# Triangular solves by halves: chunk blocks of 64 in partition halves, products in quadrants of the array

## What is computed

```python
def step(state, inp):
    r_t, w_t, k_t, v_t, kk_t, a_t = inp
    sa = jnp.einsum('bhij,bhj->bhi', state, -kk_t)
    state = (state * w_t[:, :, None, :] + sa[..., None] * (kk_t * a_t)[:, :, None, :]
             + v_t[..., None] * k_t[:, :, None, :])
    return state, jnp.einsum('bhij,bhj->bhi', state, r_t)
```

## Time and profile before

| | |
|---|---|
| runs of the kernel | 4231.69, 4227.73, 4236.51 us (median 4231.69) |
| the profiled execution | 4219.72 us, its span 4217.9 us |
| busy: PE, PEld, DVE, ACT, POOL | 91%, 78%, 63%, 38%, 15% of the span |
| granted TensorE clock, mean | 0.974 of 2.4 GHz |
| `rwkv_core` in layer 0 | 1966.1 to 2070.1 us of the span |
| `rwkv_core` in layer 1 | 3125.6 to 3223.9 us of the span |

### The profile page before, as it was taken

One profiled execution on the slowest core, in us unless ns is written; L12 is line 12 of the kernel. 1 busy time (PEld: TensorE's weight loads), 2 busy tenths in 40 slices (PEclk: granted clock), 3 DMA queues, 4 the chain that ended last, 5 costly groups with the idle time before them and its releaser, 6 DMA issues. The chain is left out here.

```text
span 4217.9 us, 62645 instructions
## 1 busy us (share of the span) xinstructions
PE 3827.2 (91%) x23712; PEld 3274.3 (78%) x23712; DVE 2652.3 (63%) x5252; ACT 1614.2 (38%) x3540; POOL 629.5 (15%) x665
## 2 busy tenths in 40 slices
PE   6999998999999999998999889888889998998887
PEld 4788765788788867897878888777778788887776
DVE  6878556677755556555346666776563476677774
ACT  3222536322332345442225444444322254444443
POOL 1100000000000000000000144444300001444442
PEclk9999998999999999998999999999999999999999
DMA  5554211354433311542033699999820346999998
GB/s 213 201 189 169 77 40 51 106 193 165 136 138 131 129 72 33 199 180 100 21 130 137 240 419 419 420 419 419 371 80 27 124 150 251 419 419 419 419 419 336
DMA packets 135053, 905.05 MB, mean 215 GB/s; under 512 B 14855, under 2 KB 15879, under 8 KB 35168
## 3 DMA queue, kind: packets, MB, share of 16 engines
q0 software_dynamic: 95552, 620.97, 36.5%
q1 hardware_dynamic: 39200, 280.08, 18.5%
HBM read 899.90 MB, written 5.28 MB: 215 GB/s over the span
## 5 line engine op out<-in xcount | busy, mean ns | idle before, releaser
L2533 PE MATMUL ps<-arena 128*128 128x128 f32 x6560 | 845.7, 285 | 155.9 <-ACT arena L2597 154.8
L2533 PEld LDWEIGHTS ps<-arena 128*128 128x128 f32 x6560 | 795.0, 197 | 217.9 <-ACT arena L2597 212.4
L2688 DVE CUSTOM_DVE_ANT_0 arena<-arena 128x1024 f32<-128x1024 f32 x410 | 502.5, 1226 | 325.9 <-DMA arena<-peer_uv,arena 325.2
L630 DVE TENSOR_TENSOR w_lo<-wt,w_hi 128x1024 fp32r<-128x1024 f32 x388 | 475.2, 1225 | 327.4 <-ACT w_hi L612 302.1
L2660 POOL DMA_INDIRECT arena<-peer_uv,arena x410 | 441.4, 1077 | 1579.1 <-DVEq L2651 988.1
L665 PE MATMUL ps<-h_hi,w_hi 128*128 128x512 f32 (+1 forms) x1744 | 643.5, 371 | 30.9 <-DVEq L631 19.2
L612 ACT ACTIVATE w_hi<-wt 128x1024 fp32r<-128x1024 f32 x388 | 407.6, 1058 | 626.7 <-PE ps L665 598.1
L665 PE MATMUL ps<-h_hi,w_lo 128*128 128x512 f32 (+1 forms) x1744 | 635.4, 366 | 0.0
L665 PE MATMUL ps<-h_lo,w_hi 128*128 128x512 f32 (+1 forms) x1744 | 594.1, 368 | 11.7 <-DVE h_lo L759 10.8
L454 PE MATMUL ps<-hT,wt 128*128 128x256 f32 x1632 | 404.4, 385 | 4.8 <-DVE hT L543 3.8
L665 PEld LDWEIGHTS ps<-h_hi,w_hi 128*128 128x128 f32 x1744 | 332.4, 191 | 93.5 <-issue 23.3
(11 more groups left out here) (347 smaller groups left out, 5510.7 us busy)
## 6 DMA issues: line engine op xcount, KB each, us to landing
wt<-wstream SPq DMA_DIRECT2D x262, 1024.0 KB, 4.8
ada_t<-adastream POOLq DMA_DIRECT2D x133, 512.0 KB, 3.6
arena<-peer_uv,arena POOLq DMA_INDIRECT x410, 20.2
arena<-adastream POOLq DMA_DIRECT2D x11, 512.0 KB, 26.6
bias_by_query<-bias_by_distance POOLq DMA_DIRECT2D x1, 4096.0 KB, 16.7
arena<-bias_by_query POOLq DMA_DIRECT2D x1, 3072.0 KB, 11.8
xT<-tokens SPq DMA_DIRECT2D x1, 2048.0 KB, 15.2
cst<-consts SPq DMA_DIRECT2D x1, 1816.0 KB, 9.1
```

What stands on the lines that cost most here:

```text
L630: self.step(self.dve.tensor_tensor(lo, raw_group(g), hi.bitcast(F32), ALU.subtract))
L2533: ins = pe.matmul(y_banks(t)[m // 4][:, (m % 4) * P:(m % 4 + 1) * P], row[:, D + m * P:D + (m + 1) * P], diag[n % DIAGS], start=s == 0 and ...
L2688: dve.tensor_tensor_reduce(u, u, ztok[:, t], 1.0, 0.0, ALU.mult, ALU.add, hbuf[:, t, s:s + 1]).then_inc(dot_ready.sem, 1)
```

## The change

The two chunks of a tile are stored one under the other: chunk c of a chain lies in partitions 64c to 64c+63, so that a chain is 128 partitions x (4 heads x 64 columns), and the zero quarters are gone. Every product of a chain is then 8 matmuls of 64 x 64 x 64 (u = 0..3, c = 0, 1) instead of 4 of 128 x 128 x 128. Chunk c uses rows 64c.. and output partitions 64c.. of the array, a quadrant on its diagonal, and writes into the bank of its own: the rings CR_ and CD_ have two slots of two banks each, in place of four banks each. ACT and DVE take such a pair of banks out in two instructions of 64 partitions x 256 columns. The transpose becomes a matmul with XT as the stationary and the identity as the moving operand. A gram makes both g of a tile at once: 16 matmuls (32 records) where two grams had 4 (8 records) each. Masks have 64 columns. The masks that produce `lrb` and `lrk` still write the wide form, with the zeros (`masked_wide`), since the next stage reads them so. All buffers of the stage now lie in the arena. The table of constants that is loaded at the start is 384 columns narrower.

```diff
-    ("level", LEVELS * P), ("before", P), ("upto", P), ("window", QT * TOK), ("cmp", QT * N_CMP),
+    ("level", LEVELS * CH), ("before", CH), ("same", CH), ("upto", P), ("window", QT * TOK), ("cmp", QT * N_CMP),
...
+        CR_ = ring("core_a", [ps[:, 4:6], ps[:, 6:8]])
+        CD_ = ring("core_d", [ps[:, 0:2], ps[:, 2:4]])
+        ROWS = [slice(i * CH, (i + 1) * CH) for i in range(2)]
         CHAINS = [(t, g) for t in range(2) for g in range(2)]
-        LATER = [(name, c) for name in ("ka", "br", "kr") for c in CHAINS]
+        LATER = [(name, t) for name in ("ka", "br", "kr") for t in range(2)]
...
-            def gram(a, b, t, g):
-                for u in range(4):
-                    mm(bank[:, u * P:(u + 1) * P], a[r, u, t * P:(t + 1) * P], b[r, u, t * P:(t + 1) * P],
-                       inc=D_.full if u == 3 else None)
+            def gram(a, b, t):
+                for u in range(4):
+                    for c in range(2):
+                        x = slice(t * P + c * CH, t * P + (c + 1) * CH)
+                        for g, r in enumerate(ROWS):
+                            mm(banks[ROWS[c], g, u * CH:(u + 1) * CH], a[r, u, x], b[r, u, x],
+                               inc=CD_.full if u == 3 and c and g else None)
-            def into(r, a, b):
-                for u in range(4):
-                    mm(bank[:, u * P:(u + 1) * P], a[:, u, :], b(u), inc=r.full if u == 3 else None)
+            def by_rows(ring_of, a, b):
+                pe.wait_ge(ring_of.free, ring_of.given_back())
+                banks = ring_of.claim()
+                for u in range(4):
+                    for c, r in enumerate(ROWS):
+                        mm(banks[r, c, u * CH:(u + 1) * CH], a[r, u, :], b(u, c, r), inc=ring_of.full if u == 3 and c else None)
...
-                    ins = pe.transpose(bank[:, u * P:(u + 1) * P], XT[c[0]][c[1]][:, u, :], ident)
+                by_rows(CR_, XT[t][g], lambda u, c, r: ident[r, c * CH:(c + 1) * CH])
...
-                    into(A_, LTL[t][g], lambda u: X[t][g][:, u, :])
-                    if coming:
+                    by_rows(CR_, LTL[t][g], lambda u, c, r: X[t][g][r, u, :])
+                    if coming and i % 2:
...
-                    into(D_, Y[t][g], lambda u: XT[t][g][:, u, :])
+                    by_rows(CD_, Y[t][g], lambda u, c, r: XT[t][g][r, u, :])
...
-            def four_out(dst, ready):
-                step(act.activation(dst, bank.rearrange("p (a b) -> p a b", b=P), ACT.Copy))
+            def rows_out(dst, ready=None):
+                for c, r in enumerate(ROWS):
+                    ins = act.activation(dst[r], banks[r, c, 0:4 * CH].rearrange("p (u j) -> p u j", j=CH), ACT.Copy)
+                if ready:
+                    step(ins)
...
-                step(dve.tensor_tensor(dst, bank4(bank), four(const(mask)), ALU.mult))
+                for g in range(2):
+                    step(dve.tensor_tensor(dsts[g], banks[:, g, 0:4 * CH].rearrange("p (u j) -> p u j", j=CH),
+                                           four(const(mask)), ALU.mult))
...
-                step(dve.tensor_tensor(dst, dst, bank4(bank), ALU.add))
+                for c, r in enumerate(ROWS):
+                    ins = dve.tensor_tensor(dst[r], dst[r], banks[r, c, 0:4 * CH].rearrange("p (u j) -> p u j", j=CH), ALU.add)
+                step(ins)
```

More of the change, by code:

```diff
@@ L1704, in act_rwkv_core @@
-            for t, g in CHAINS:
-                act.wait_ge(A_.full, A_.filled())
-                bank = A_.take()
-                act.activation(by_group(utok, t)[:, :, g, :], bank[:, 0:256].rearrange("p (a b) -> p a b", b=HD),
-                               ACT.Copy).then_inc(A_.free, 1)
+                    rows_out(Y[t][g], act_ready)
+            for t in range(2):
+                for g in range(2):
+                    rows_out(W1[t][g], act_ready)
+                act.wait_ge(CR_.full, CR_.filled())
+                banks = CR_.take()
+                act.activation(xat[:, :, t, :].rearrange("p u (c j) -> p u c j", j=CH),
+                               banks[:, :, 0:4 * CH].rearrange("p c (u j) -> p u c j", j=CH), ACT.Copy).then_inc(CR_.free, 1)
@@ L1723, in added, with masked @@
-            def added(dst):
-                dve.wait_ge(D_.full, D_.filled())
-                bank = D_.take()
-                step(dve.tensor_tensor(dst, dst, bank4(bank), ALU.add))
-                dve.sem_inc(D_.free, 1)
+                return ap.unsqueeze(1).to_broadcast([P, 4, CH])
+            def masked(dsts, mask):
+                dve.wait_ge(CD_.full, CD_.filled())
+                banks = CD_.take()
+                for g in range(2):
+                    step(dve.tensor_tensor(dsts[g], banks[:, g, 0:4 * CH].rearrange("p (u j) -> p u j", j=CH),
+                                           four(const(mask)), ALU.mult))
+                dve.sem_inc(CD_.free, 1)
@@ new lines, in masked_wide @@
+            def masked_wide(dst, mask, t):
+                dve.wait_ge(CD_.full, CD_.filled())
+                banks = CD_.take()
+                wide = [P, 4, 2, CH]
+                for g in range(2):
+                    step(dve.tensor_tensor(
+                        dst[:, t, g::2].rearrange("p u (c j) -> p u c j", j=CH),
+                        banks[:, g, 0:4 * CH].rearrange("p (u j) -> p u j", j=CH).unsqueeze(2).to_broadcast(wide),
+                        const(mask).rearrange("p (c j) -> p c j", j=CH).unsqueeze(1).to_broadcast(wide), ALU.mult))
+                dve.sem_inc(CD_.free, 1)
@@ L1729, in level_of @@
+            def added(dst):
+                dve.wait_ge(CD_.full, CD_.filled())
+                banks = CD_.take()
+                for c, r in enumerate(ROWS):
+                    ins = dve.tensor_tensor(dst[r], dst[r], banks[r, c, 0:4 * CH].rearrange("p (u j) -> p u j", j=CH), ALU.add)
+                step(ins)
+                dve.sem_inc(CD_.free, 1)
             def level_of(t, g, level):
-                step(dve.tensor_tensor(LTL[t][g], LT[t][g], four(const("level", level, P)), ALU.mult))
+                step(dve.tensor_tensor(LTL[t][g], LT[t][g], four(const("level", level, CH)), ALU.mult))
```

124 lines of the change are left out of this document (49 added, 75 removed).

## The result

The change made the kernel faster by more than I forecast, and by more than my range allowed. The median after is 4176.55 us (4 runs, 4170.52 to 4179.04); that of before, with one more run, is 4233.94. The ratio is 0.9864, 95% interval 0.9847 to 0.9882. I had said 4211.

A forecast was written before the change was run, and what follows sets the result against it. A plain level was about half PE's, half DVE's. 79.0 us a layer plus 0.55 x 20.9 for half clock gave 181 for both layers against 202.4; saving 21.4 less 1.5, so 4211 us, range 4182 to 4236.

The forecast's parts named there:

- The sum at full clock: rwkv_core a layer: start-up 12.3, gram levels 39.6, plain level 10.9, level 5 7.1, tail 9.1; together 79.0 us.
- Which clock?: Step on PE's clock in rwkv_core: PE idles more often, so half clock for some 55% of the stage.
- the sign that I had named for being wrong: PEclk in the stage above 0.9 would show the forecast wrong; it expected near 0.7.
- the price that I put on half clock: rwkv_core wholly at half clock takes 99.9 us a layer against 79.0 at full, 20.9 more.
- rival (1): The clock holds: both layers of rwkv_core at 79.0, a saving of 44 us, kernel at 4187; chance 0.21.
- The 1.5 for `rwkv_out`: Next stage would begin at half clock where it now begins at full, taking 1.5 us off the saving.
- the difference of 12.0 between profile and median: Profiled execution of before, 4219.7, lies 12.0 us under the runs' median; the same difference was assumed after.
- The grams: Levels 1 to 3: 12 grams of 1.09 us in line become 6 of 1.06; 39.6 us against 49.5.
- (2): Rival: half clock throughout rwkv_core, 2 x 99.9 us, a saving of 2.6, kernel at 4229; chance 0.18.
- (4): Rival: the change does nothing because DVE is the bound; plain levels nearly so, 10.9 against 11.36; no separate chance.
- (3): Rival: the 0.033 us matmul rate fails; with half clock 148 us a layer, kernel at 4325; chance 0.09.
- the bound of 0.82 a product: Upper bound for a 16-record product at full clock, 0.82 us against 0.53 taken; some 3 us a level.

The follow-up runs named there:

- a_one_by_one: Kernel after, a product's eight matmuls ordered four of chunk 0, then four of chunk 1, so quadrants don't alternate; stage 84.8 and 84.0 us, kernel 4187.1.
- a_doubled: Kernel after, each product of turns, A and D products, W1 and u made twice into the same banks; stage 89.4 and 91.1 us, median 4198.9.
- a_idle: Kernel after, PE held ahead of each stage until ACT made 24 added copies; stage 77.8 and 76.9 us, kernel 4202.1.
- a_early_grams: Kernel after, a level's two grams moved behind the third and fourth turn ahead of it; stage 71.4 and 72.3 us, median 4164.0.
- a_events: Kernel after, levels and tail without engines waiting for their own copy, addition or mask before signalling; stage 67.5 and 71.0 us, median 4158.7.
- a_kept: Kernel after, three added matmuls of 128 columns ahead of each turn while PE waits for DVE; stage 88.7 and 92.9 us, median 4200.6.
- b_kept: Kernel before, two added matmuls of 512 columns in each of four start-up waits; stage 100.2 and 108.9 us, median 4225.3.

## Why the prediction was wrong

**The sum at full clock: right.** 79.0 us a layer forecast; 76.7 measured, with some 10.7 us at half clock in it. The product's 0.53 (0.50), ACT's 0.96, DVE's 0.84 and 1.66 all held. Four parts were off by over 1 us, in both directions and partly by where I cut them: the start-up (11.0 for 12.3), the gram levels (38.5 for 39.6), level 5 (8.5 for 7.1) and the tail (7.7 for 9.1). That their errors nearly cancel is in part luck.

**The step that failed: "Which clock?"** I wrote: "PE is idle more often, not less ... So I expect it at half clock for more of the stage than before, some 55%." It was 14% (10.7 of 76.7), in four stages of two profiles, at PEclk 0.93: the sign that I had named for being wrong, above 0.9, came true. a_one_by_one and a_doubled show that the inference does not carry: the one is busier than after at a lower clock, the other busier at a higher one. And the price that I put on half clock, 0.21 us for each us, was 0.08 in a_idle. I had written down the very rows (ACT's 0.96 and DVE's 1.66 against a product of 1.06) by which a slow PE hides, but priced only the first products of each row of four as if nothing could absorb them. In numbers: the forecast added 0.55 x 20.9 = 11.5 us a layer for the clock, 23 in both. At 0.08 the 21.4 us at half clock cost 1.7. This term made 21 of the missing 34.5 us. The share was the larger error: 0.14 x 20.9 would have been 2.9 a layer, at my own price. Why the clock held is not known. My rival (1), 4187, was this case, and I gave it 0.21.

**Smaller terms.** The full-clock sum was too high by 2.3 us a layer plus the 0.9 that half clock cost: 6 in both. The 1.5 for `rwkv_out` did not come (it starts at full clock). And the stage of before is usually longer than the profile I read: 208.8 in its second profile against 202.4, 6.4 us which the medians contain. I also wrote 4211 where 4231.7 - 21.4 + 1.5 is 4211.8. 21 + 6 + 1.5 + 6.4 is 35, where 34.5 was missing. That it closes so well is luck: the rest of the kernel took 4015.6 and 4018.2 us in the two profiles of before and 4023.8 and 4015.0 in those of after, and the difference of 12.0 between profile and median, which I had carried over from before, was -2.5 in after's first profile. Only the term of the clock is larger than all that.

**The grams: the right place, the wrong reasons.** I said the gain was there because 12 grams of 1.09 became 6 of 1.06. They became 6 of 0.5, since all four quadrants overlap. And some 0.36 of each gram's and of each A product's 1.09 had been the change of shape. Neither showed in my gram levels (38.5 measured, 39.6 forecast), because ACT's copies and DVE's wide masks stand over them: a_early_grams, which only moves the grams, takes off nearly all that their removal does.

**Rivals (2) to (4).** (3) fell: the rate held over 1440 records. a_one_by_one gives its milder form, the bound of 0.82 a product: 84.8 us, still far under before. At like clock it cost 0.5 to 0.8 us a level, where I had priced some 3. The Trainium skill ("TensorE: Matmul & The Clock Gate", Back-to-back issue gap) names about 62 ns for each matmul where software decodes it. The 16 records of a product would take 1.0 us by it and took 0.50, and the 32 of a gram took 0.5, 16 ns each; the measurement decides against such a cost here. (4) was half right: a plain level went from 11.36 to 11.0.

## What to carry to other kernels

Ask what half clock costs where the engine waits anyway, before asking how long it lasts: here it cost 0.37 us for each us where TensorE set the pace, and 0.08 where ACT and DVE did, each from one comparison. Once TensorE is cheap, look at the copies: the Trainium skill ("TensorEngine Tiling (Array Packing)", PSUM Bottleneck) says that the copy out of PSUM may become the bottleneck, and here taking out the waits around copies and additions took 14.9 us off the two stages with no matmul changed. Read two profiles of the kernel before: a stage that takes 98 us in one may take 105 in the next. And price an edit in one stage by that stage: the rest of this kernel moved by 12 us from one execution to another.

## What was unexpected of the hardware

- The order of matmuls over quadrants decides their rate. The weight loads of 16 records that stand alone take 0.82 us when eight in a row stay in a quadrant, 0.57 when two quadrants alternate. A gram of 32 records takes 1.2 us quadrant by quadrant, and some 0.5 round all four.
- Alternating between matmuls of 64 x 128 and of 128 x 128 costs some 0.36 us at each change.
- A busier order can have the lower clock: 73.3 us busy of 84.8 at PEclk 0.84, where 54.9 of 76.7 had 0.93. It need not: 81.5 of 89.4 had 0.98.
- In layer 1 of a_events PE stood still for 0.85 us with nothing in the profile to wait for, between two stretches of a gram level, and the masks behind it came later by as much; in layer 0 the same place ran through. The cause was not tried, and it is part of why layer 1 took 3.5 us more there:

```profile
3127.06 3.46 PE L456 MATMUL ps<-arena 64*64 64x64 f32 x120 [0.16 <-ACT arena L1689]
...
3131.36 0.81 PE L456 MATMUL ps<-arena 64*64 64x64 f32 x24 [0.85 <-issue]
```

What sets the granted clock in this stage stays open: neither PE's busy share nor the matmuls added in a_kept and b_kept foretold it.
